# Two layers of a streaming encoder on one core: where the value tokens, the memory transposes, the identity load and the weight buffers stand

## What is computed

```python
def trunk_layer(x, ...):
    h = rmsnorm(x, g_norm[0])
    fq, fk, fv, ff, cq, ckv, kpe, hq, hf, hi, hg, ga, gb, gc = split(h @ w_in)
    f_logf = log_sigmoid(ff + b_fox)                  # forget gate of the first branch
    # first branch ("fox"): softmax(q k^T + cum_q - cum_k) v, cum = cumsum(f_logf);
    # for the new tokens cum = cumsum(concat(cached logf, f_logf))
    # second branch ("mla"): latent attention; third ("hgrn"): gated linear recurrence
    merged = sum(sigmoid(gate_b) * (o_b @ w_branch[b]) for b in range(3))
    x = x + rmsnorm(merged @ w_out, g_norm[1])
    qx = rmsnorm(x, g_norm[2]) @ w_xq                 # cross-attention into 256 memory tokens
    ox = attend(qx, mem_prompt @ w_mem_k, mem_prompt @ w_mem_v)   # new tokens: a cached memory
    x = x + rmsnorm(ox @ w_xo, g_norm[3])
    u = square(relu(rmsnorm(x, g_norm[4]) @ w_up)) @ w_down
    x = x + rmsnorm(u, g_norm[5])
```

## Time and profile before

| | before |
|---|---|
| median of 3 runs | 2743.57 us (2743.19 to 2744.48) |
| profiled execution | 2743.87 us, of it a span of 2742.0 us from the first to the last instruction |
| TensorE matmuls | 2551.7 us, 93% of the span |
| GpSimd / VectorE / ScalarE | 1210.9 / 1045.0 / 707.3 us (44%, 38%, 26%) |
| granted clock of TensorE, mean | 0.966 of 2.4 GHz |

### The profile page before, as it was taken

One profiled execution on the slowest core, in us unless ns is written; L12 is line 12 of the kernel. 1 busy time (PEld: TensorE's weight loads), 2 busy tenths in 40 slices (PEclk: granted clock), 3 DMA queues, 4 the chain that ended last, 5 costly groups with the idle time before them and its releaser, 6 DMA issues.

```text
span 2742.0 us, 43279 instructions
## 1 busy us (share of the span) xinstructions
PE 2551.7 (93%) x18670; PEld 2386.0 (87%) x18670; DVE 1045.0 (38%) x1596; ACT 707.3 (26%) x1571; POOL 1210.9 (44%) x700
## 2 busy tenths in 40 slices
PE   8899999998988899999998999999998887999997
PEld 7878977997888789999898789689888887999997
DVE  5442222478623341221373411324786144211223
ACT  2053133135312430010121522322253134210111
POOL 3312510665465245665543034126643732565663
PEclk9999999999999999999999999999999998999998
DMA  5313410330242123323234133113202421223321
GB/s 178 111 38 102 109 41 16 85 90 24 77 125 85 39 62 88 91 85 89 81 101 120 39 89 91 42 32 85 74 24 93 130 80 32 77 85 89 90 85 56
DMA packets 354533, 214.59 MB, mean 78 GB/s; under 512 B 22316, under 2 KB 347240, under 8 KB 353704
## 3 DMA queue, kind: packets, MB, share of 16 engines
q1 hardware_dynamic: 320632, 179.86, 23.1%
q10 hardware_dynamic: 33712, 31.97, 3.7%
HBM read 196.09 MB, written 15.71 MB: 77 GB/s over the span
## 4 chain that ended last, share of the span: by engine, by line
PE 83%; DVE 8%; ACT 4%; issue 3%; POOL 2%; DMA 0%; ACTq 0%; SPq 0%; DVEq 0%; POOLq 0%
PE psum L719 20%; PE psum L717 20%; PE psum L718 20%; PE psum L788 2%; PE psum L827 2%; PE psum L729 2%; PE psum L1110 1%; PE psum L998 1%; POOL w_lo L652 1%; PE psum L921 1%; PE psum L747 1%; PE psum L749 1%; PE psum L748 1%; DVE square_sum_and_rs L2020 1%; PE psum L762 1%
## 5 line engine op out<-in xcount | busy, mean ns | idle before, releaser
L650 POOL CAST w_hi<-w_raw 128x1024 fp32r<-128x1024 f32 x318 | 337.7, 1062 | 1382.5 <-PE psum L719 1204.9
L652 POOL TENSOR_TENSOR w_lo<-w_raw,w_hi 128x1024 fp32r<-128x1024 f32 x318 | 811.6, 2552 | 25.5
L717 PE MATMUL psum<-h_hi,w_hi 128*128 128x272 f32 x2720 | 791.1, 291 | 18.9 <-POOL w_lo L652 15.1
L719 PE MATMUL psum<-h_hi,w_lo 128*128 128x272 f32 x2720 | 788.4, 290 | 0.0
L718 PE MATMUL psum<-h_lo,w_hi 128*128 128x272 f32 x2720 | 783.8, 288 | 0.0
L717 PEld LDWEIGHTS psum<-h_hi,w_hi 128*128 128x128 f32 x2720 | 513.9, 189 | 24.0 <-issue 20.9
L718 PEld LDWEIGHTS psum<-h_lo,w_hi 128*128 128x128 f32 x2720 | 514.4, 189 | 0.7 <-issue 0.5
L719 PEld LDWEIGHTS psum<-h_hi,w_lo 128*128 128x128 f32 x2720 | 512.8, 189 | 0.0
L717 PE MATMUL psum<-r_hi,w_hi 128*128 128x272 f32 x1696 | 494.2, 291 | 6.2 <-DVE hE L2114 3.3
L719 PE MATMUL psum<-r_hi,w_lo 128*128 128x272 f32 x1696 | 495.8, 292 | 0.0
L718 PE MATMUL psum<-r_lo,w_hi 128*128 128x272 f32 x1696 | 491.8, 290 | 0.0
(11 more groups left out here) (380 smaller groups left out, 3593.7 us busy)
## 6 DMA issues: line engine op xcount, KB each, us to landing
w_raw<-in_w_in SPq DMA_DIRECT2D x116, 512.0 KB, 3.8
w_raw<-in_w_up SPq DMA_DIRECT2D x64, 512.0 KB, 4.0
w_raw<-in_w_down SPq DMA_DIRECT2D x64, 512.0 KB, 3.9
w_raw<-in_w_branch SPq DMA_DIRECT2D x24, 512.0 KB, 3.4
w_raw<-in_w_out SPq DMA_DIRECT2D x16, 512.0 KB, 3.9
x_kept<-x SPq DMA_DIRECT2D x2, 2176.0 KB, 8.9
x<-x_kept SPq DMA_DIRECT2D x2, 2176.0 KB, 9.7
fKc<-in_cache_fox_k ACTq DMA_DIRECT2D x4, 1024.0 KB, 7.8
```

Of the source, the lines that this page charges most:

```text
L650: nc.gpsimd.tensor_copy(w_hi[:, at % SPLIT, :], raw[:, at % RAW, :]).then_inc(high_split, 1)
L652: nc.gpsimd.tensor_tensor(w_lo[:, at % SPLIT, :], raw[:, at % RAW, :], w_hi[:, at % SPLIT, :].bitcast(F32), ALU.subtract).then_inc(weights ...
L717: pe.matmul(dst, whi[:, k, :], hi[:, k, c0:c1], start=k == 0, stop=False)
L719: last = pe.matmul(dst, wlo[:, k, :], hi[:, k, c0:c1], start=False, stop=k == kt - 1)
```

## The change

- `SPLIT` goes from 2 to 3 and `RAW` from 4 to 2 (the same space). SyncE's first two loads stay ahead of the loop, whose start is now written as 2.
- The memory transposes use the banks T, O, A0 and A1 in place of T and O in turn.
- Memory product 6 moves from behind `out` 5 to behind `out` 7, ahead of 7; its weight slot moves with it.
- On TensorE and in the plan, the value tokens stand ahead of the cached gate's product. On VectorE, the two memsets of `fq` and the copy to `fq_new` move ahead of the copies of the key tokens, and the copies of the value tokens ahead of the scans of the cached gate.
- The load of the identity and ones moves from SyncE's queue, behind the five vectors, to the head of ScalarE's queue, ahead of its table load.

```diff
--- before.py
+++ after.py
@@ -45,7 +45,7 @@
 MB = N_MEM // P
 CB = PAST_LEN // P
 CACHED = PAST_LEN + DEC_SEQ
-RAW, SPLIT = 4, 2
+RAW, SPLIT = 2, 3
 MLP_GROUPS = D_FF // D_MODEL
 
 
@@ -88,7 +88,7 @@
 
 
 
-MEMORY_AT = {(2, 3): (0,), **{("out", n): (n + 1,) for n in range(6)}, ("out", 7): (7,)}
+MEMORY_AT = {(2, 3): (0,), **{("out", n): (n + 1,) for n in range(5)}, ("out", 7): (6, 7)}
 
 
 GATES = {
@@ -235,7 +235,7 @@
             gemm(("br", b, 2 * j), ("br", b, 2 * j + 1))
             if memory and j == 2:
                 for i in range(4):
-                    tr(("memT", i))
+                    t.add(END_BANKS[i], ("memT", i))
             for i in MEMORY_AT.get((b, j), ()):
                 gemm(memory_name(i))
 
@@ -244,8 +244,8 @@
     tokens("fk")
     for tb in range(TB + 1):
         tr(("flogf", tb))
+    tokens("fv")
     tr(("clogf", 0)), tr(("clogf", 1))
-    tokens("fv")
     attention("fox", FOX_HEADS)
     for g in range(2):
         for b in ("A0", "A1", "T"):
@@ -625,7 +625,7 @@
             load(sp, S["clogf"][:, :, :], clog.rearrange("(b p) h -> p b h", p=P), "clogf")
 
         def sp_layer(sp, l):
-            for s in range(0 if l else SPLIT, N_SLOTS):
+            for s in range(0 if l else 2, N_SLOTS):
                 load_slot(sp, l, s)
                 if s == SLOT_OF["fk", 0]:
                     if l:
@@ -898,6 +898,8 @@
                 name = ("flogf", tb)
                 pe.matmul(bank_free(pe, name)[0:c1 - c0, 0:FOX_HEADS], S["flogT"][:, c0:c1],
                           ident[0:FOX_HEADS, 0:FOX_HEADS], start=True, stop=True).then_inc(fill_sem(name), 1)
+            emptied(pe, ("fv", 3))
+            tokens(pe, "fv", [R["fvT"][:, n, :] for n in range(4)])
             pe.wait_ge(DMA["clogf"], since(DMA["clogf"], 16))
             for j in range(2):
                 name = ("clogf", j)
@@ -906,8 +908,6 @@
                     last = pe.matmul(bank[0:FOX_HEADS, P * b:P * b + P], S["clogf"][:, 4 * j + b, :], ident,
                                      start=True, stop=True)
                 last.then_inc(fill_sem(name), 1)
-            emptied(pe, ("fv", 3))
-            tokens(pe, "fv", [R["fvT"][:, n, :] for n in range(4)])
             gate_product(pe, ("fox", -1))
             pe.wait_ge(ncum_ready, since(ncum_ready, 1))
             emptied(pe, ("fv", "tok", TB))
@@ -1895,6 +1895,11 @@
                 V.scalar_tensor_tensor(e0, flog, -1.0, flog, ALU.mult, ALU.max).then_inc(ff_vector, 1)
                 v.wait_ge(ff_scalar, since(ff_scalar, 1))
                 V.scalar_tensor_tensor(flog, flog, 0.0, e1, ALU.min, ALU.subtract).then_inc(ff_vector, 1)
+                for j in range(2):
+                    r = slice(64 - 64 * j, 128 - 64 * j)
+                    step(v, V.memset(S["fq"][r, :, :].rearrange("p (m t) n -> p m t n", t=2)[:, :, j, :], 0.0))
+                emptied(v, ("fq", 3)), emptied(v, (("fq", 2), 1))
+                step(v, V.tensor_copy(S["fq_new"][:, :, :], S["fq"][:, :, SEQ:NT]))
                 to_tokens(v, "fk", S["fk_tok"], M["fk_s"], 512)
                 for tb in range(TB + 1):
                     rows = P if tb < TB else DEC_SEQ
@@ -1910,6 +1915,7 @@
                 step(v, V.tensor_copy(high, e1[:, 0:SEQ]))
                 step(v, V.tensor_tensor(parts[LOW_ROWS:LOW_ROWS + FOX_HEADS, :], e1[:, 0:SEQ], high.bitcast(F32),
                                         ALU.subtract))
+                to_tokens(v, "fv", S["fv_tok"], S["fv_s"], 512)
                 for j in range(2):
                     name = ("clogf", j)
                     filled(v, name)
@@ -1919,12 +1925,6 @@
                     emptied(v, name)
                 V.tensor_tensor_scan(ncums[:, PAST_LEN:CACHED], e0[:, 0:DEC_SEQ], flog[:, SEQ:NT],
                                      ncums[:, PAST_LEN - 1:PAST_LEN], ALU.mult, ALU.subtract).then_inc(ncum_ready, 1)
-                for j in range(2):
-                    r = slice(64 - 64 * j, 128 - 64 * j)
-                    step(v, V.memset(S["fq"][r, :, :].rearrange("p (m t) n -> p m t n", t=2)[:, :, j, :], 0.0))
-                emptied(v, ("fq", 3)), emptied(v, (("fq", 2), 1))
-                step(v, V.tensor_copy(S["fq_new"][:, :, :], S["fq"][:, :, SEQ:NT]))
-                to_tokens(v, "fv", S["fv_tok"], S["fv_s"], 512)
                 v.wait_ge(DMA["x_out"], since(DMA["x_out"], 16))
                 gate(v, ("fox", -1))
                 attention(v, "fox", cst[:, K_CAUSAL:K_CAUSAL + P], FOX_DIM)
@@ -2209,7 +2209,6 @@
         def _(sp):
             layer_now[0] = 0
             sp_vectors(sp, 0)
-            sp.dma_start(cst[:, 0:K_CAUSAL], A["constants"][:, 0:K_CAUSAL]).then_inc(ident_loaded, 16)
             load_slot(sp, 0, 0), load_slot(sp, 0, 1)
             sp_columns(sp, 0)
             sp.dma_start(cst[:, K_CAUSAL:K_END], A["constants"][:, K_CAUSAL:K_END]).then_inc(consts_loaded, 16)
@@ -2266,6 +2265,7 @@
 
         @block.scalar
         def _(act):
+            act.dma_start(cst[:, 0:K_CAUSAL], A["constants"][:, 0:K_CAUSAL]).then_inc(ident_loaded, 16)
             act.preload_act_table_set("natural_log_exp_and_others")
             for tb in range(TB):
                 act.dma_start(S["x_tok"][:, tb, :], A["x_prompt"][0, P * tb:P * tb + P]).then_inc(x_arrived[tb], 16)
```

## The result

| | before | after |
|---|---|---|
| median | 2744.03 us (4 runs, 2743.19 to 2744.67) | 2720.72 us (4 runs, 2717.73 to 2724.97) |
| ratio, 95% interval | | 0.9915 (0.9904 to 0.9927) |
| profiled execution | 2743.87 us, span 2742.0 | 2721.17 us, span 2719.4 |

The change gains 23.3 us. The prediction had 2712 us, with a gain of 31.1: the direction held, the time lies in the range 2696 to 2722, and the gain is 8 us smaller than forecast. The question of the experiments is which term of the sum is wrong.

The account below looks back on a forecast made before the run. TensorE, busy 93% of the span, was taken as the bound, so gains come only from its pauses or low clock. Per layer 15.3 us, twice 30.6, plus 0.5 gave 31.1 off 2743.9: 2712 us, range 2696 to 2722.

Parts of the forecast that it names:

- A: Value tokens ahead of the cached sums: gate product starts and ends earlier, 5.5 us per layer gained (4.4 to 7.7).
- B: Memory transposes in four banks: the first out product starts earlier, 4.6 us per layer gained (3.6 to 6.5).
- C: Three split buffers in the out stage: all six waits for GpSimd go, 8.4 us per layer gained (7.6 to 9.2).
- D: Recurrence, fourth head: the third buffer's earlier split delays VectorE's last L2020, 2.3 us per layer lost (0 to 2.4).
- E: Behind the out stage: a third split stands beside VectorE's L1726 pair, 0.9 us per layer lost (0 to 1.5).
- F: Kernel start: identity load on ScalarE's queue makes weights land earlier, 0.5 us gained once (-0.7 to 1.5).
- the rival in which they hold the scores: Behind the gate product: cached sums, now last, hold the scores, so value tokens gain nothing; 2723 us, chance 0.07.
- the refill: Out stage, part of C: the refill behind each pause for GpSimd, perhaps 0.27 us, goes with the waits.
- Two raw buffers: Weight loads: two raw buffers instead of four cost nothing, as loads land 3.9 us after start at the median.
- The sign named as wrong: GpSimd waiting for w_raw landings in the profile would show the forecast wrong.
- the rivals that starve a stage: Two raw buffers starve the out stage (2729 us, chance 0.08) or the dense stages too (about 2917, chance 0.04).

Follow-up runs that it names:

- tokens: Kernel before with only the value tokens moved ahead of the cached gate's sums: 2734.19 us, ratio 0.9964.
- banks: Kernel before with only the memory transposes in four banks: 2735.87 us, ratio 0.9965.
- split3h: Kernel before with three split and two raw buffers, gate slot (2, 7) still waiting for the product two slots back: 2723.97 us, ratio 0.9928.
- split3: Kernel before with only three split and two raw buffers, memory product 6 staying behind out 5: 2736.69 us, ratio 0.9970.
- hold: Changed kernel with the split of gate slot (2, 7) waiting for the product two slots back, as before the change: 2707.76 us, ratio 0.9867.
- hold2: Changed kernel with the splits of gate slot (2, 7) and xq slot 2 waiting for the product two slots back: 2706.69 us, ratio 0.9865.
- ident: Kernel before with only the load of the identity and ones at the head of ScalarE's queue: 2744.64 us, ratio 1.0002.
- base: Kernel before run once more without an edit: 2743.96 us, ratio 1.0000.
- same: Changed kernel run once more without an edit: 2717.53 us, ratio 0.9906.
- mem6: Changed kernel with memory product 6 back behind out 5: 2720.29 us, ratio 0.9915.
- hold4: Same as hold3, and the split of gate slot (2, 6) waits until the last scaling is done: 2708.27 us, ratio 0.9868.
- hold3: Same as hold2, and the split of slot fq 2 also waits for the product two slots back: 2705.45 us, ratio 0.9867.

## Why the prediction was right in direction and too large

**The sum against single runs.**

| term | forecast | measured by times |
|---|---|---|
| A | 11.0 | 9.7 (tokens) |
| B | 9.2 | 7.8 (banks) |
| C | 16.8 | 19.4 (split3h) |
| D | -4.6 | -12.7 (split3 against split3h); -13.0 and -9.8 (the changed kernel, twice, against hold) |
| E | -1.8 | -1.1 (hold against hold2, not separated) |
| F | 0.5 | -0.7 (ident, not separated from 0) |
| sum | 31.1 | 22.4, with -12.7 for D |

The whole change measured 23.3, and 26.4 in the second set of its runs (2743.89 - 2717.53). **The mis-sized term is D**, by 5 to 8 us. The single terms carry a few us of noise each, and C and D share split3h, so that their sum comes near 23.3 proves little by itself. That the time lies in the range is in part luck: D was far outside its bounds (0 to 4.8 for both layers), C came out above its own (15.2 to 18.4) and paid for a part of it, and the measured time stands 1.3 us below the upper end.

**A** was right. The first value copy starts at 117.06 (forecast 116.8, and the stage begins 0.2 late), the gate product at 122.84 (123.6), its result is read 6.42 later (6.5), the scans end at 124.9, under the product: the rival in which they hold the scores is out. Per layer it was 5.3 to 6.9 in the profiles. The clock decided between the ends, as said, but not always the same way. In the first layer of the changed kernel the 16 plain matmuls took 2.24 us, in its second layer 3.54, in the first layer of tokens 3.43; the earlier trace rows had 3.50. Where they were short, A was large (6.6 at 2.24, 5.3 at 3.54). The window of these matmuls in the changed kernel:

```profile
120.60:122.90 2.30, 2.30 (x18) 1.57 (x17) 1.50 (x2) 0.00 (x0) 0.00 (x0) 0.83 0.21 78
```

And in tokens:

```profile
119.60:123.10 3.50, 3.50 (x18) 1.99 (x17) 1.89 (x2) 0.00 (x0) 0.00 (x0) 0.54 0.48 181
```

The Trainium skill's rule on transposes and the clock ("TensorE: Matmul & The Clock Gate", Part 4: PE-mode transpose: a transpose doesn't count as activity for the clock as a matmul does), on which the prediction leaned for its choice, is neither shown nor refuted by these two: behind the same transposes the clock was mostly back in one and still low in the other.

**B** was right: the memory product waits 2.01, `out` 0 starts at 769.33 (forecast 769.5); 4.4 to 4.8 per layer (4.6).

**C** was right and a little small: with one low stretch at its beginning the stage is 7.4 shorter, without it 9.0 (forecast 8.4). The six waits were 7.6 of it, and the other 1.4, or 0.24 for each pause, is what the prediction called the refill (perhaps 0.27). It also takes away the pause of 1.26 in front of `out` 0, which I had not counted (split3h: 1.4 in both layers against `base`); in the whole change B's wait for `U` stands in its place.

**Two raw buffers** were right. The sign named as wrong did come: GpSimd waits for landings in the `out` stage of the changed kernel, but no wait of TensorE follows from it, and the rivals that starve a stage are out (GpSimd's waits between 755 and 862 us, changed kernel):

```profile
POOL w_hi L650 <- DMA w_raw<-in_w_mem_v: 2.2, 1, 2.2
POOL w_hi L650 <- DMA w_raw<-in_w_out: 0.8, 1, 0.8
```

**D** had the right mechanism, place and local price, and the wrong total. The step that failed is "I take 2.3; bounds 0 (VectorE gets in first) to 2.4 (a whole subtraction)": it prices the delayed L2020 and stops there. TensorE had one pause of 1.0 here and got a second of 2.38; behind it the clock fell to 0.51 over busy matmuls, while without it (hold) the clock stays at 1.00. The stage is longer by 3.8 to 5.7 per layer (after, same, split3 and mem6) than in kernels without D whose recurrence in front is alike. I had let pauses pull the clock down in A, and not here. The Trainium skill's rule on the port that VectorE and GpSimd share ("SBUF — State Buffer", Who interferes with whom) is borne out by the rows shown: 2.6 us beside a split, 0.4 without, in six kernels.

**E** was right locally (1.0 to 1.7 per layer) and nearly nothing in the end; its origin was named wrongly: it comes with the move of memory product 6, for which the prediction had nothing, and that nothing holds for the time only (mem6).

**F**: nothing that can be told from 0. The first product begins at 19.66 in place of 20.02, but in ident at 20.09: the `r_lo`, now earlier, stand beside the second split, which the prediction had as the reason of its lower bound, and the split takes 4.3 us in place of 3.5. GpSimd in the timeline of the changed kernel:

```profile
15.23 1.54 POOL L650 CAST w_hi<-w_raw 128x1024 fp32r<-128x1024 f32 x1
16.85 2.71 POOL L652 TENSOR_TENSOR w_lo<-w_raw,w_hi 128x1024 fp32r<-128x1024 f32 x1
```

And in the kernel before:

```profile
15.82 1.04 POOL L650 CAST w_hi<-w_raw 128x1024 fp32r<-128x1024 f32 x1
16.94 2.36 POOL L652 TENSOR_TENSOR w_lo<-w_raw,w_hi 128x1024 fp32r<-128x1024 f32 x1
```

The third split stands beside the `r_lo`, too, and they are longer for it. VectorE in the changed kernel:

```profile
13.78 12.72 DVE L1717 SCALAR_TENSOR_TENSOR r_lo<-x,vectors,r_hi 128x544 fp32r<-128x544 f32 x8 [0.97 <-ACT r_hi L1274]
```

In ident, which has no third split there:

```profile
14.32 9.73 DVE L1717 SCALAR_TENSOR_TENSOR r_lo<-x,vectors,r_hi 128x544 fp32r<-128x544 f32 x8 [0.98 <-ACT r_hi L1274]
```

But the key tokens begin no earlier in ident (0.6 later than in the kernel before), so the third split isn't what takes F away. From the first product to the key tokens the changed kernel and ident take 88.7 us at a mean clock of 0.83 over the first 18 us of it, before 88.2 at 0.86, `same` 87.2 at 0.92. This spread between executions is larger than F, and `tokens`, which has no F, shows it as well (87.5).

**What stays open.** In the changed kernel's first profile the attention costs 3.4 and 7.6 and gives 1.5 and 1.4 back. `same` shows that the places aren't fixed, `base` that the first layer's part needs no edit at all. In the second layer the low stretch was absent in base, ident, split3h and hold4 and present in the other edited kernels. What decides it wasn't found; that D brings it is not shown, as tokens and banks have it without D. A sum made against one profile can't be better than these few us.

## What to carry to other kernels

A buffer more lets work start earlier everywhere, and where it lands beside the engine that the bound engine waits for, it can cost more than it brings: follow the freed work to each place where it may now run (here a recurrence, the end of a stage and of a layer), and keep the old condition at these places. A pause of the bound engine is priced with the clock behind it, not by its length alone. When one profile is the basis, take a second one of the same kernel before you explain a few us in a stretch that nothing touches.

## What was not expected of the hardware

- One more pause of TensorE, of 2.38 us, close behind one of 1.0, cost 3.8 to 5.7 us: the clock was at 0.51 behind it.
- The clock can be at 0.50 over 6.8 to 10.2 us in which TensorE is busy throughout (28 to 45 matmuls, 52 at 1.00 in 6.8 us), at places that differ between executions of one kernel; the changed kernel's runs spread over 8.3 us (2716.70 to 2724.97), those of split3h over 1.0.
- VectorE operations with two inputs took longer beside a GpSimd split: L2020 2.57 in place of 0.42, two sums of squares 3.80 in place of 1.44, eight `r_lo` 12.72 beside two splits and 9.73 beside one. The kernel before already had such a place at the end of the first layer, worth some 3 us (hold3).
